# Mixers of a two-part transformer stack: S5 tables made in the feed-forward, the RWKV inverse on 64x64 blocks, the S5 scan begun in it

## The reference, cut to what matters

```python
def step(state, inp):                       # RWKV-7, 256 tokens one after the other
    r_t, w_t, k_t, v_t, kk_t, a_t = inp
    s_kk = jnp.einsum('bhvk,bhk->bhv', state, kk_t)
    state = (state * w_t[:, :, None, :] - s_kk[..., None] * (kk_t * a_t)[:, :, None, :]
             + v_t[..., None] * k_t[:, :, None, :])
    return state, jnp.einsum('bhvk,bhk->bhv', state, r_t)
...
lam_bar = jnp.exp(lam * dt)                 # S5, complex
b_bar = ((lam_bar - 1.0) / lam)[..., None] * lax.complex(b_re, b_im)
bu = jnp.einsum('gpi,btgi->btgp', b_bar, ug)
_, states = lax.associative_scan(combine, (broadcast(lam_bar), bu), axis=1)
y = jnp.real(jnp.einsum('gip,btgp->btgi', c_mat, states)) + d_skip * ug
```

## Time and profile before

| | us |
|---|---|
| median of 3 runs (lowest, highest) | 3060.18 (3057.88, 3070.09) |
| the profiled execution: its own time | 3064.51 |
| the profiled execution: its span | 3062.7 |
| PE busy in the span | 2660.0 (87%) |
| DVE busy | 1954.6 (64%) |
| ACT busy | 1517.5 (50%) |
| GpSimd busy | 87.4 (3%) |

### The profile page before, as it was taken

One profiled execution on the slowest core, in us unless ns is written; L12 is line 12 of the kernel. 1 busy time (PEld: TensorE's weight loads), 2 busy tenths in 40 slices (PEclk: granted clock), 3 DMA queues, 4 the chain that ended last, 5 costly groups with the idle time before them and its releaser, 6 DMA issues. The chain is left out here.

```text
span 3062.7 us, 36509 instructions
## 1 busy us (share of the span) xinstructions
PE 2660.0 (87%) x13005; PEld 2171.5 (71%) x13006; DVE 1954.6 (64%) x2382; ACT 1517.5 (50%) x1868; POOL 87.4 (3%) x96
## 2 busy tenths in 40 slices
PE   3889985897856958899897887999999899999998
PEld 3678773786755647678765766777788677777777
DVE  2555616555479954455546446987445698898987
ACT  2544424443221034344435435776444577777776
POOL 0000002000011300000010000000000000000000
PEclk8999977998878879899988987999999999999999
DMA  9335431454000044255432425998455699999996
GB/s 245 127 126 192 159 87 42 151 192 140 28 8 1 1 164 145 76 162 190 152 129 69 139 69 173 367 330 316 154 189 179 216 359 329 328 361 326 363 330 223
DMA packets 333110, 561.72 MB, mean 183 GB/s; under 512 B 21865, under 2 KB 126504, under 8 KB 332872
## 3 DMA queue, kind: packets, MB, share of 16 engines
q1 hardware_dynamic: 333000, 560.22, 54.3%
HBM read 555.99 MB, written 4.19 MB: 183 GB/s over the span
## 5 line engine op out<-in xcount | busy, mean ns | idle before, releaser
L1150 DVE TENSOR_TENSOR weights_split<-ring,weights_split 128x1024 fp32r<-128x1024 f32 x676 | 819.1, 1223 | 262.2 <-ACT weights_split L1145 226.6
L1225 PE MATMUL ps<-weights_split,expert_split 128*128 128x512 f32 x3864 | 910.4, 393 | 23.8 <-DVE expert_split L1321 17.8
L1145 ACT ACTIVATE weights_split<-ring 128x1024 fp32r<-128x1024 f32 x676 | 714.8, 1061 | 348.3 <-PE ps L1225 337.9
L1225 PEld LDWEIGHTS ps<-weights_split,expert_split 128*128 128x128 f32 x3864 | 719.7, 188 | 189.5 <-DVE weights_split L1150 35.3
L289 DVE TENSOR_TENSOR weights_split<-ring,weights_split 128x2048 fp32r<-128x2048 f32 x182 | 413.5, 2273 | 477.8 <-ACT weights_split L280 477.8
L280 ACT ACTIVATE weights_split<-ring 128x2048 fp32r<-128x2048 f32 x182 | 344.8, 1896 | 438.5 <-PE ps L460 279.1
L459 PE MATMUL ps<-normed_split,weights_split 128*128 128x512 f32 x1248 | 447.8, 401 | 39.4 <-PEq L342 39.4
L460 PE MATMUL ps<-normed_split,weights_split 128*128 128x256 f32 x1248 | 354.3, 284 | 0.0
L459 PEld LDWEIGHTS ps<-normed_split,weights_split 128*128 128x128 f32 x1248 | 240.5, 193 | 95.3 <-issue 41.4
L365 PE MATMUL ps<-weights_split,hidden_split 128*128 128x512 f32 x1032 | 241.8, 390 | 8.0 <-DVE hidden_split L553 8.0
L460 PEld LDWEIGHTS ps<-normed_split,weights_split 128*128 128x128 f32 x1248 | 240.6, 193 | 1.4
(11 more groups left out here) (357 smaller groups left out, 2484.5 us busy)
## 6 DMA issues: line engine op xcount, KB each, us to landing
ring<-moe_w_gate SPq DMA_DIRECT2D x112, 1024.0 KB, 5.2
ring<-moe_w_up SPq DMA_DIRECT2D x112, 1024.0 KB, 5.3
ring<-moe_w_down SPq DMA_DIRECT2D x112, 1024.0 KB, 5.1
ring<-mlp_w_up SPq DMA_DIRECT2D x32, 1024.0 KB, 5.4
ring<-mlp_w_down SPq DMA_DIRECT2D x32, 1024.0 KB, 4.9
ring<-xa_w_kv SPq DMA_DIRECT2D x16, 1024.0 KB, 5.3
ring<-moba_w_qkv SPq DMA_DIRECT2D x12, 1024.0 KB, 11.1
ring<-da_w_qkv SPq DMA_DIRECT2D x12, 1024.0 KB, 5.2
```

The costliest lines, as they stand in the source:

```text
L1145: nc.scalar.activation(split_piece(p, 0), ring_piece(p), ACT.Copy).then_inc(high.sem, 1)
L1150: nc.vector.tensor_tensor(split_piece(p, 1), ring_piece(p), split_piece(p, 0).bitcast(F32), ALU.subtract)\
L1225: last = nc.tensor.matmul(ps[:, banks[half][tt], :], stationary(s, k, tt), split_piece(p, i)[:, kk * NW:(kk + 1) * NW], start=(opens and n ...
```

## The change

- The table work (angles, coefficients, cos and sin) goes from the inverse into the second feed-forward: on ACT and DVE right behind the hidden values of a chunk, chunks 0 to 13. The tables are made in the arena, saved to a tensor in HBM in the final norm's stage (128 x 4464 floats, issued ahead of the gain), and loaded into the ring in the stage with the loras. SP waits for the save ahead of the loras' loads.
- The input and output matrices of S5 are made by GpSimd in the stage with the loras (`prepare`) and turned in the pairs stage.
- The masks have 64 columns. Pairs are made as 64x64 blocks in four quadrants of PE, eight DVE operations of 512 elements mask them. The inverse has 64x64 blocks, both halves of the tokens in two quadrants; its DVE and ACT operations have 256 elements instead of 512.
- The first five S5 scan steps are in the inverse, one behind the last batch of each level; the first four projections too. Projections and outputs are issued for two state tiles at a time, their products alternating. N1 and N2 have four buffers instead of two.
- The recurrence: the products that don't need the state come first in G, the state products come ahead of the outputs O, O has its own bank, the state has two buffers, GS and US are no longer cleared.
- The late parameter rows are turned in the stage of the index scores.

The diff, cut to its core:

```diff
@@ mlp, act and dve, behind the halves of the hidden values
+                    if beside:
+                        beside.tables_act(e, c)
...
+                    if beside:
+                        beside.tables_dve(e, c)
@@ rwkv_s5
     def sp(e):
+        e.wait_ge(*mixer.saved.at(16))
         e.dma_start(LORA_W[0:64, :], l0["rw_w_up_2"]).then_inc(*lora_landed.up(16))
...
-    stage(core, pe=pe, act=act, dve=dve)
+    mixer.place(UT, YT[:, 4:8, :], [a(14592 + 512 * i, 512) for i in range(4)])
+    stage(core, sp=mixer.load, pe=pe, act=act, dve=dve, pool=mixer.prepare)
...
+        for w_ in range(NU // 4):
+            if w_ >= 2:
+                e.wait_ge(*masked.at(2 * w_ - 2))
+            for tt in range(TT):
+                for i, src in enumerate((BT, KT)):
+                    for hp, ch in ((0, 0), (1, 1), (0, 1), (1, 0)):
+                        rows, tok = slice(64 * hp, 64 * hp + 64), slice(CH * ch, CH * ch + CH)
+                        at_ = (2 * tt + i) * P
+                        last = nc.tensor.matmul(ps[tok, 2 * (w_ % 2) + hp, at_:at_ + P],
+                                                src[rows, w_, tt * P + CH * ch:tt * P + CH * ch + CH],
+                                                AR[rows, w_, tt, :, tok], start=True, stop=True)
...
+        mixer.turn(e)
@@ inverse
+    blocks = [(slice(CH * ch, CH * ch + CH), slice(CH * u, CH * u + CH)) for u in range(4) for ch in range(2)]
...
-            mixer.tables_dve(e, n)
+            if n % 4 == 3:
+                mixer.scan_dve(e, n // 4)
...
             nc.gpsimd.tensor_tensor(q(LM[:, n % 2, :]), LT(b), bc(c(f"level{s}"), 1, 4), ALU.mult).then_inc(*masked.up())
+            if n % 4 == 1 and n > 4:
+                mixer.scan_pool(e, n // 4 - 1)
+        mixer.scan_pool(e, 4)
...
     def pe(e):
+        mixer.scan_project(e, 0)
+        mixer.scan_project(e, 1)
...
-                for u in range(4):
-                    cols = slice(u * P, (u + 1) * P)
-                    last = nc.tensor.matmul(ps[:, n % 2, cols], LM[:, n % 2, cols], X[:, b, cols], start=True, stop=True)
+                for tok, cols in blocks:
+                    last = nc.tensor.matmul(ps[tok, n % 2, cols], LM[tok, n % 2, cols], X[tok, b, cols],
+                                            start=True, stop=True)
...
+            if n in (10, 18):
+                mixer.scan_project(e, 2 + n // 16)
@@ recurrence, pe
+            e.wait_ge(*u_copied.at(c + 1))
+            if c < NCH - 1:
+                for j in range(J):
+                    cols = slice(j * P, (j + 1) * P)
+                    nc.tensor.matmul(ps[:, 1, cols], BN[tok, tt, cols], US[tok, cols], start=True, stop=False)
+                    last = nc.tensor.matmul(ps[:, 1, cols], KN[tok, tt, cols], VN[tok, tt, cols], start=False, stop=True)
+                last.then_inc(*s_done.up())
+                mixer.scan_project(e, (4, 5, 7)[c])
+                mixer.scan_out(e, (1, 2, 4)[c])
@@ recurrence, dve
+        for c in range(NCH):
+            mixer.scan_dve(e, FIRST + 3 * c)
+            if c < NCH - 1:
+                e.wait_ge(*s_done.at(c + 1))
+                if c:
+                    e.wait_ge(*o_done.at(c))
...
+            for s in (1, 2):
+                mixer.scan_dve(e, FIRST + 3 * c + s)
@@ S5
     def load(self, e):
+        e.wait_ge(*self.saved.at(16))
+        e.dma_start(self.core.ring[:, :, :].rearrange("p r n -> p (r n)")[:, 0:ST * T], self.kept[:, 0:ST * T])\
+            .then_inc(*self.loaded.up(16))
+        e.dma_start(self.small, self.kept[:, ST * T:]).then_inc(*self.landed.up(16))
...
+        if n == 4:
...
+            for level in self.LEVELS[0:3]:
+                self.double(e, level, 0, ST)
+        if n in (5, 6, 7):
+            self.double(e, self.LEVELS[n - 2], 0, ST)
+        if n in (8, 9):
+            self.double(e, self.LEVELS[6], (n - 8) * (ST // 2), ST // 2)
+        if 10 <= n < 14:
+            self.double(e, self.LEVELS[7], (n - 10) * (ST // 4), ST // 4)
...
+    def scan_out(self, e, p):
...
+        e.wait_ge(*self.back.at(m0 + 2))
+        for k, (w_, src, part) in enumerate(terms):
+            for m in (m0, m0 + 1):
+                j = m % 4
+                cols = slice(32 * j, 32 * j + 32)
+                last = core.nc.tensor.matmul(core.ps[cols, 3, ct % 2 * T:(ct % 2 + 1) * T], w_[:, ct, cols],
+                                             src[:, m % 4, part * T:(part + 1) * T], start=(k == 0), stop=(k == 3))
@@ program, final norm of the first block
     def sp(e):
+        e.dma_start(mixer.kept, mixer.tables).then_inc(*mixer.saved.up(16))
         e.dma_start(gain, w["final_norm"].partition_broadcast(P)).then_inc(*gain_landed.up(16))
```

418 lines of the change are left out of this document (201 added, 217 removed).

## The result

The changed kernel takes 3035.76 us (median of 4 runs, 3029.94 to 3038.16), the kernel before 3062.47 (4 runs, 3057.88 to 3070.09): a ratio of 0.9894, 95% interval 0.9871 to 0.9917, so 25 to 40 us less, 26.7 by the medians. The forecast was 3018, 42 us less, with a range of 2990 to 3042: the time lies inside, and the gain is two thirds of the one forecast. The profiled execution lasted 3029.94 us, the fastest of the four, with a span of 3028.0: 34.7 less than the span of before.

A forecast was written before the change was run, and what follows sets the result against it. PE was taken to bound the feed-forward, PE and DVE nearly full in the recurrence, the mixer stages running alone. Pairs -2, inverse -50, recurrence -21, feed-forward +22, save and reload +7, rest +2: -42 us, 3018 us; range 2990 to 3042.

The forecast's parts named there:

- The stops of the feed-forward: Second feed-forward: table work beyond a 1.49 us margin delays the weight split and stops PE; +22 us for the part.
- The gain behind the save: Final normalization: the gain's transfer waits behind the 2.29 MB save on the same queue; +7 us, between 0 and 12.
- Quadrants side by side: Inverse: eight 64x64 products in two quadrants overlap, taking 0.5 us for the 0.89 of four 128x128 products.
- strips don't help: Rival: 64x64 products in two quadrants follow one another, inverse 80 us, recurrence 78, pairs 18, whole 3060; chance 0.06.
- tables nearly free: Rival: DVE's 72 idle us in the feed-forward absorb the tables, costing no more than 2 us; 2998 us, chance 0.12.
- The pairs with four quadrants by turns: Pairs stage: with four 64x64 products at once the pairs need about 4 us of PE; stage about 10 us, -2 us.
- PE waiting in each level for the mask behind GpSimd's sums: Inverse: the next mask comes 4.3 us after the scan began, so PE gets no further than one group.
- The recurrence: Recurrence stage: DVE's work plus a 3.3 us first wait, 2 us at the end, +3 for clock; 69 us for 90.
- one or two of these stops: Second feed-forward: that many PE stops cost a further 1 us, as the next group runs slower.
- The inverse: Inverse stage: 64x64 blocks in two quadrants, tables gone, scan steps between levels; 55 us for 105, -50 (45 to 65).
- three times 0.7: Inverse: allowance in us for PE's clock falling after it idles 3 us in each level.
- the level period of 9.5: Inverse: us per level, a 4.5 us scan on DVE, then 5.0 for two more PE steps and alternating updates.

The follow-up runs named there:

- the last experiment: Eight further groups of 64x64 products, results unread, at the end of PE's part of the inverse, against the kernel combining four moves: 2995.65 us, ratio 0.9783.
- the four ahead of the sums' move: Changed kernel without table work, with tables spread over both idle stretches, gain issued before save, or doublings on GpSimd: 3012.2, 3006.6, 3034.2, 3026.8 us.
- the two on the recurrence: Changed kernel with two S5 scan steps ahead of the first state update, or S5 products of two tiles not by turns: 3036.3, 3042.4 us.
- one tile after the other: Changed kernel with the S5 projection and output products of two state tiles issued tile by tile instead of by turns: 3042.4 us.
- the kernel without tables: Changed kernel without ScalarE's and VectorE's table work in the second feed-forward, constant fills on GpSimd standing in: 3012.2 us.
- four moves together: Changed kernel with tables spread over both idle stretches, gain before save, GpSimd's sums behind the fourth mask, inverse scan steps in three parts: 2986.94 us, ratio 0.975.

## Why the prediction was right, and where its terms were off

**Right in its mechanism, part by part.**
- The stops of the feed-forward. Predicted for chunks 3 to 13: 1.3, 4.8, 0, 2.3, 1.7, 1.2, 2.7, 0.6, 2.3, 0.6, 2.3. Measured: 1.28, 4.56, 0, 2.21, 1.34, 1.17, 2.39, 0, 2.76, 0.24, 2.28. Three rows (the split's duration, where the hidden values end, where PE begins) gave the series. Two things in this are luck. The first 1.3 doesn't follow from the formula with the 0.9 to 1 us that the text has for chunk 2 (4.4 - 1.49 - 1 = 1.9); the measured work of chunk 3 was 3.97 us, and the stops ahead of it 0.27 and 0.93. And the alternation at the end is that of five profiles; in the other three the last stops are 1.23 to 1.29 each, since a low clock stood behind the stop of chunk 6. The rule survives that, if the time lost at 1.2 GHz is subtracted with the stop: chunk 10 has 4.35 - 1.49 - 2.39 - 1.6, below zero, and stopped for 0 and not for 0.6.
- The gain behind the save: +5.6 for +7, shown by exchanging the two.
- Quadrants side by side: 0.47 us a group for 0.5. The rival "strips don't help" is out, and so is "tables nearly free".
- The pairs with four quadrants by turns: 64 products in 1.98 and 2.30 us of PE, 4.3 together, for the 4 us of the prediction. The Trainium skill, "TensorEngine Tiling (Array Packing)", Tiling Modes, calls 64x64 tiles four independent ones; the trace agrees (a record of these products takes 0.031 us, one of the inverse with half the columns in two quadrants 0.029).
- PE waiting in each level for the mask behind GpSimd's sums: shown by moving the sums.
- The recurrence: 70.4 for 69, with DVE's first wait 5.2 for 3.3 and the last sums' 3.8 for 2. The first wait was long since PE began the stage at half clock: at full clock, in the last experiment, it was 2.97. (Two of the recorded sums don't add up: DVE's parts give 61.0 and not 60.1, the first chunk's 8.5 and not 8.8. Neither moves the 66.)

The two large terms missed the same way, the feed-forward by 5.5 us and the inverse by 5.8 in this profile; pairs, normalization and the stages between gave 5 back. What kept the forecast inside its range is the width of the range.

**The term of the clock in the feed-forward was mis-sized.** The prediction allowed 1 us for "one or two of these stops". Three were followed by half clock, 5.6 us in all, since each time 9 to 11 products of 128x512 or 128x256 ran at twice their time before the clock was back. The 1 us had been read from the earlier trace rows, a group of small products that ended before the low clock did (the group behind it, at 952.80, took 1.36 us to the next start in place of 0.89). A second term was put at nothing: the 0.24 us that a stop costs beyond its length, 2.6 us for 11.

**The inverse was put too low, by 6 us in this profile and by more in others.** Seven profiles have this inverse (the changed kernel's, the four ahead of the sums' move, the two on the recurrence; in "one tile after the other" the projections' products stand in another order): 61.3, 62.8, 64.7, 64.8, 66.1, 66.2, 66.2 us, with PE's clock at 0.87, 0.85, 0.80, 0.80, 0.78, 0.78, 0.78. So 55 missed by 6 to 11. The mis-sized terms are "three times 0.7" for the clock, and the level period of 9.5. The mask was there for PE 4.65 us after the scan's start in place of 4.3 (935.74 to 940.39, and twice more). From there to the next scan it was 5.1 us, as forecast (5.2), only where PE ran at full clock; it was 7.6 where three groups ran at half clock and a projection, which the period left out, stood in PE's queue behind them (1.1 us; 2.0 at half clock), and 6.7 where four groups ran at half clock. The conflict of DVE and GpSimd that the prediction had named and left out is there, 0.53 us for DVE in three steps, but no stop of PE is put down to it: where PE stood, it stood for the mask. In the profile of the changed kernel the levels took 9.8, 12.2 and 11.3 us; in that of the kernel without tables 11.3, 15.1 and 11.3, in the long one eight groups and a projection at half clock. DVE's busy time is 38.1 in all seven, PE's goes from 39.5 to 44.7: what differs between them is the clock alone. This may also answer for a part of the distance between the profiled execution (3029.9) and the median (3035.8).

**What the forecast missed as a design question.** It took the period of 9.5 us as given and compared it with the time before. It did not ask what the twenty steps and the five scan steps would cost one behind the other, which its own figures nearly had (5.0 + 28 + 5 x 4.5, 56 us): what it hoped for from the interleaving, and less than that gave.

**Open.** Why the clock was never low behind the stop of 2.76 us, in eight profiles, and always low behind those of 2.25 to 2.42, in five; the two kinds of profile say only that it goes with what stood ahead. And why the recurrence, with the same code, ran at 0.84 to 0.85 in the five kernels that share the change's inverse and recurrence (70.4 us each time) but at 0.64, 0.77, 0.80 and 0.78 behind four other inverses (80.9, 75.2, 73.0, 74.2), and at 0.80 in "four moves together" (73.0). That it depends on what PE did before is shown by the last experiment for the first chunk only.

## What to carry to other kernels

Before work is moved under another stage, write down for one period of that stage where its engine stands idle, for how long, and who is late if each stretch is overrun; the sum of the idle time says nothing (72 us free, 53 us of work, 27 lost), pieces that fit the stretches cost 0.6. An in-order engine that serves two chains (GpSimd with masks and sums, SyncE's queue with save and gain) should get first what somebody waits for now: exchanging save and gain was worth 4.6 us, moving the sums 11 to 16 in the inverse, of which the recurrence took 10.5 back. And a stage that became shorter can leave the next one at a lower clock, so count the stages together.

## What the runs showed of the hardware

- Products of 64x64 in two quadrants, float32, two records each: eight in 0.47 us at 2.4 GHz by turns, 0.57 with each quadrant's four in a row, 0.86 by turns at 1.2 GHz. The pairs, with four quadrants by turns, took 1.98 us for 32 products of 64x64x128 (64 records).
- Strips of 32 rows overlap even when the products of one tile stand together (two projections 1.07 us either way); strips of 32 columns lose half of the gain (1.85 by turns, 2.74 not).
- GpSimd's 128x1024 products beside the feed-forward took 2.3 to 4.3 us each in the mean of their kind, DVE's two-input SBUF operations 24 to 87% more in the mean (a split 2.29 us or up to 4.46), its PSUM operation nothing. In the inverse a DVE operation of 128x512 took 1.21 us beside a mask of GpSimd, 0.68 without one.
- Each stop of PE in the feed-forward cost some 0.24 us beyond its length, and 1.5 to 2.5 us more where the granted clock was 0.50 behind it.
- Of two transfers on one queue the second, smaller one landed after 8.6 us behind 2.29 MB and after 4.5 ahead of it.
